# The preparation of the odd mixer, moved from a block of its own into the input projection ahead of it

## The chip, the cores and the metric

The kernel runs on one NeuronCore of a Trainium2 chip. The metric is the device time of one execution in microseconds (us), the median of several runs.

## The reference, cut to what matters

A trunk of two layers is stepped once for 576 tokens: one prompt of 512 and eight samples of 8. Each layer is a feed-forward half step, a mixer and another feed-forward half step. The mixer of the second layer, the odd one, is the place of the change. Its input projection `h @ w_in_odd` gives queries, keys, values and output gates for two kinds of heads, and in 24 further columns a low-rank input of the decays and the pre-activations of two gates:

```
q, k, v, gk_lr, z = _split(pc, C_WIDTHS)
gk = log_sigmoid(gk_lr @ w_gk2 + b_gk) / 16              # log decays, summed over each chunk
o_c = (_rms(gla(q, k, v, gk)) * gain_c) * silu(z)
q, k, v, i_in, f_in, o_in = _split(pd, D_WIDTHS)
f = cumsum(log_sigmoid(f_in + b_f));  m_t = max(log f_t + m_{t-1}, i_t)   # running sum and maximum
o_d = sigmoid(o_in) * (_rms(mlstm(q, k, v, i_in + b_i, f, m)) * gain_d)
```

All of it is fp32.

## The kernel before, in words

Features lie on the 128 partitions and the T = 576 tokens along the free dimension. `build` calls a chain of program blocks. `dense_chain` (L496) runs matrix products stage after stage in one block. After it come `prepare_odd` (L2865) and `odd_mixer` (L3085), each a block of its own (`nc.cleanup_on_exit()`, `nc.Block()`), and a second `dense_chain`. No instruction of a block starts before every engine, SyncE's DMA queue among them, has left the block before.

**A dense stage.** An output tile of 128 features is a unit of one or more pieces; a piece is one transfer of weights (128x1024). A product of fp32 accuracy is made of three passes: ScalarE copies the weights rounded (`split_high`, L161), VectorE subtracts to get the rest (`split_low`, L165), and TensorE multiplies low by high, high by low, high by high (L902, L904, L906), two matmuls of 288 columns each, over eight 128-row slices. The last stage is `proj_odd`, the input projection: 25 tiles, of which tile 24 (`NARROW`) holds the 24 further columns. Its first five tiles are made side by side of 288 tokens (10 pieces), the other 20 whole (20 pieces). Each engine's program is one loop over the pieces: in step i, VectorE first copies the tile that ended with piece i-1 out of PSUM (`copy_out`, L1242), then ScalarE and VectorE split the weights of piece i+2, whose place is free once piece i-1 has ended. TensorE waits at a unit for the copy of the unit three tiles back. Two units of TensorE's work therefore lie between the end of a piece and the use of what is split then.

**What else runs in the stage.** `Modulation` makes the shift, scale and gate vectors of the next sublayer: 16 transfers `w_mod` of 768 KB on SyncE's queue, from the fifth piece on, and a product after each of 16 pieces (L117), in psum banks 6 and 7. SyncE's queue runs through the transfers in order and waits at each for the place that it fills.

**`prepare_odd`.** SyncE fetches `w_gk2` (16 KB), the mixer's constants (1440 KB: masks, selections, and `resets`, the ones with zeros at which a running sum starts anew) and the samples' `m0` (L2898 to L2900). ScalarE makes silu of four tiles and sigmoid of four others (L2913, L2914; 128x2304 each), then the log-sigmoid of the forget gate as Abs, Exp, Ln (L2917 to L2921), each of the last two with an ACT_TABLE_LOAD. VectorE copies the gates' rows, makes the running sum and the running maximum (two scans of 4x576) and from them the mixer's rows. TensorE makes the inputs of the log decays (L2949: four matmuls, two tiles). For each of these two tiles in turn, VectorE shifts it (L3017), ScalarE runs Abs, Exp, Ln (L2924 to L2928), VectorE ends the log-sigmoid, scales it and makes two scans (L3020 to L3027). At the end ScalarE makes two exponentials of rows, TensorE turns rows into columns (L2954, L2956) and ScalarE copies these out (L2935, L2939).

**`odd_mixer`** takes four chunks of 128 tokens and one for the samples. TensorE's order is front(0), front(1), weights(0), outputs(0), weights(1), then for each chunk its rest and the next one's front. A front is eight transposes, fourteen products that use the constants and rows of 4 partitions, and some of 64 partitions.

## Time and profile before

| | before |
|---|---|
| median of 3 runs, us | 2833.3 (2832.71 to 2843.31) |
| the profiled execution's own time, us | 2840.6 |
| its span, first to last instruction, us | 2838.8 |
| granted TensorE clock, mean | 0.942 |
| busy share PE, PEld, DVE, ACT, POOL | 93%, 87%, 59%, 37%, 23% |
| from the last matmul of the projection to the first of the mixer, us | 2203.77 to 2246.43 |

PE is TensorE's matmul, PEld its weight load, DVE VectorE, ACT ScalarE, POOL GpSimd, SP SyncE. PEclk is the granted TensorE clock: 1.00 is 2.4 GHz and 0.50 is 1.2 GHz, the two levels that it has. The other engines' instructions keep their length at either level. In a timeline a row is one or several like instructions: start, time covered, engine, line, operation, out<-in, count, and in brackets how long the engine had been idle and what ended that.

### The profile page before, as it was taken

Reading aid. Unit: us, or ns where it says so; the run is one execution under the profiler, and the core shown is the slowest. Engines: PE = TensorE matmul, PEld = TensorE weight load, DVE = VectorE, ACT = ScalarE, POOL = GpSimd, SP = SyncE. Lnnn points to the kernel's source line nnn. Section 1 sums busy time; section 2 is a strip of 40 time slices with the busy share of each in tenths; the row PEclk is TensorE's granted clock in tenths of the full one; section 3 lists DMA queues with packets and bytes.
Section 4 is the critical chain, followed back from the end, with each engine's and each line's share of the span. In section 5 each row is a group of like instructions: output and inputs, shape, how many; then the busy total and the mean of one; then the engine's idle time right before and its main releaser. Section 6 shows DMA issues by size and latency. Waiting matters only on the chain. (4 is left out here: it accounts for less than half of the span.)

```text
span 2838.8 us, 52254 instructions
## 1 busy us (share of the span) xinstructions
PE 2638.0 (93%) x22592; PEld 2460.6 (87%) x22592; DVE 1688.3 (59%) x2345; ACT 1051.5 (37%) x1527; POOL 667.1 (23%) x502
## 2 busy tenths in 40 slices
PE   3999999999689998999999999999999498999998
PEld 0999988899378876899998999998889378999998
DVE  2787725743466646678952678852622355787824
ACT  2444414322533322444432544432421433544522
POOL 1356201000011021245510045510000121256401
PEclk7999999999679987999999999999999579999999
DMA  6233455621100013322255422255651104232324
GB/s 250 75 97 98 147 191 160 244 86 47 58 2 3 3 55 123 119 75 90 92 175 167 133 75 96 95 175 171 212 191 53 51 20 127 75 97 91 100 82 128
DMA packets 79757, 307.30 MB, mean 108 GB/s; under 512 B 9112, under 2 KB 14120, under 8 KB 77992
## 3 DMA queue, kind: packets, MB, share of 16 engines
q1 hardware_dynamic: 79528, 303.96, 32.4%
q8 instruction: 178, 2.92, 0.4%
q14 instruction: 51, 0.42, 0.0%
HBM read 293.19 MB, written 10.74 MB: 107 GB/s over the span
## 5 line engine op out<-in xcount | busy, mean ns | idle before, releaser
L165 DVE TENSOR_TENSOR weights_r<-work,weights_r 128x1024 fp32r<-128x1024 f32 (+2 forms) x300 | 392.7, 1309 | 292.9 <-ACT weights_r L161 292.3
L161 ACT ACTIVATE weights_r<-work 128x1024 fp32r<-128x1024 f32 (+2 forms) x300 | 291.4, 972 | 551.8 <-PE banks L906 334.4
L904 PE MATMUL banks<-low_r,weights_r 128*128 128x288 f32 (+2 forms) x1112 | 270.7, 300 | 0.0
L799 POOL TENSOR_TENSOR rows<-rows,consts 128x288 f32<-128x288 f32 (+3 forms) x64 | 88.7, 1386 | 692.8 <-ACT consts L1018 688.3
L902 PE MATMUL banks<-low_r,weights_r 128*128 128x288 f32 (+2 forms) x800 | 207.9, 307 | 26.4 <-DVE weights_r L165 17.7
L816 PE MATMUL banks<-h_r,weights_r 128*128 128x288 f32 x780 | 230.6, 296 | 0.9 <-DVE weights_r L165 0.9
L817 PE MATMUL banks<-big_r,weights_r 128*128 128x288 f32 x780 | 229.9, 295 | 0.0
L818 PE MATMUL banks<-h_r,weights_r 128*128 128x288 f32 x780 | 229.8, 295 | 0.0
L902 PE MATMUL banks<-h_r,weights_r 128*128 128x288 f32 (+1 forms) x824 | 198.2, 302 | 23.1 <-DVE big_r L423 22.8
L904 PE MATMUL banks<-big_r,weights_r 128*128 128x288 f32 (+2 forms) x848 | 210.0, 298 | 0.0
L165 DVE TENSOR_TENSOR ring_r<-work,ring_r 128x1024 fp32r<-128x1024 f32 (+1 forms) x108 | 148.7, 1377 | 93.8 <-ACT ring_r L161 93.4
L906 PE MATMUL banks<-low_r,weights_r 128*128 128x288 f32 (+2 forms) x800 | 201.7, 299 | 0.0
L906 PE MATMUL banks<-h_r,weights_r 128*128 128x288 f32 (+1 forms) x824 | 194.7, 298 | 0.0
L904 PEld LDWEIGHTS banks<-low_r,weights_r 128*128 128x128 f32 x1112 | 191.7, 191 | 0.2
L902 PEld LDWEIGHTS banks<-low_r,weights_r 128*128 128x128 f32 x800 | 139.7, 192 | 49.7 <-issue 25.0
L818 PE MATMUL banks<-low_r,weights_r 128*128 128x288 f32 x584 | 173.6, 297 | 0.0
L817 PE MATMUL banks<-low_r,weights_r 128*128 128x288 f32 x584 | 173.2, 297 | 0.0
L902 PEld LDWEIGHTS banks<-h_r,weights_r 128*128 128x128 f32 x824 | 138.9, 189 | 38.9 <-issue 31.0
L816 PE MATMUL banks<-low_r,weights_r 128*128 128x288 f32 x584 | 172.3, 295 | 0.0
L161 ACT ACTIVATE ring_r<-work 128x1024 fp32r<-128x1024 f32 (+1 forms) x108 | 104.1, 963 | 147.9 <-PE banks L818 111.0
L816 PEld LDWEIGHTS banks<-h_r,weights_r 128*128 128x128 f32 x780 | 146.6, 188 | 1.6 <-DVE weights_r L165 1.6
L818 PEld LDWEIGHTS banks<-h_r,weights_r 128*128 128x128 f32 x780 | 146.9, 188 | 0.0
(557 smaller groups left out, 7160.7 us busy)
## 6 DMA issues: line engine op xcount, KB each, us to landing
work<-w_ff_dram SPq DMA_DIRECT2D x118, 512.0 KB, 3.7
h<-w_mod_dram SPq DMA_DIRECT2D x48, 768.0 KB, 5.2
work<-w_down_dram SPq DMA_DIRECT2D x66, 512.0 KB, 3.6
consts<-w_ff_dram SPq DMA_DIRECT2D x58, 512.0 KB, 3.6
work<-w_mod_dram SPq DMA_DIRECT2D x32, 768.0 KB, 9.3
work<-w_in_even_dram SPq DMA_DIRECT2D x24, 512.0 KB, 3.8
big_buf<-w_mod_dram SPq DMA_DIRECT2D x16, 768.0 KB, 6.0
consts<-w_down_dram SPq DMA_DIRECT2D x22, 512.0 KB, 3.6
```

Of the source, the lines that this page charges most:

```text
L161: return act.activation(high, raw, ACT.Copy)
L165: return engine.tensor_tensor(low, raw, high.bitcast(F32), ALU.subtract)
L799: pool.tensor_tensor(k.rows[:, c], k.rows[:, c], k.square[:, c], ALU.add).then_inc(added, 1)
L816: pe.matmul(out, low[:, w], x_high, start=j == 0, stop=False)
L817: pe.matmul(out, high[:, w], x_low, start=False, stop=False)
L818: last = pe.matmul(out, high[:, w], x_high, start=False, stop=j == KT // 2 - 1)
L902: pe.matmul(out[a], low[:, w], x[a][0], start=begins, stop=False)
L904: pe.matmul(out[a], high[:, w], x[a][1], start=False, stop=False)
L906: last = pe.matmul(out[a], high[:, w], x[a][0], start=False, stop=closes)
```

## The change

`prepare_odd` is gone, and with it one block. Its work is spread over steps 12 to 24 of the projection's 30 pieces, by a class `OddGates`. The narrow tile is made first (`row` starts at `NARROW`), so that it is there after piece 5. Silu and sigmoid are made tile by tile as ScalarE takes the tile out of PSUM (`gate_out`), in place of VectorE's copy. The two log-decay tiles are handled as one of 1152 columns in ScalarE's three operations, and share psum pair 3 with each other. The resets are made by GpSimd. `w_gk2` and `m0` are fetched early in the stage, behind a wait for the last residual add of the stage before (`taken`). The constants are fetched in two parts at the end of the transfers, the second once the last piece that used their place has ended; the mixer's first product that reads them waits for both. The second slot of the modulation's weights is moved elsewhere in SBUF.

```diff
...
-        self.row = [(m + (UP_FIRST if kind == "up" else 0)) % n for m in range(n)]
+        self.row = [(m + {"up": UP_FIRST, "proj_odd": NARROW}.get(kind, 0)) % n for m in range(n)]
...
+class OddGates:
...
+        self.x, self.soft_x = k.arena[:, 6 * D:6 * D + 2 * T], at(11, 2)
+        self.col_rows, self.resets16, self.resets = at(13), at(14), at(15)
+        self.lf, self.soft, self.fsum = row(at(16)), row(at(17)), row(at(18))
...
+    def load(self, sp):
+        sp.dma_start(self.w2, self.k.io["w_gk2"]).then_inc(self.loaded, 16)
+        sp.dma_start(self.m0, self.k.io["mm_in"]).then_inc(self.loaded, 16)
+    def store(self, sp):
+        sp.wait_ge(*self.q.after("dve", "m_last"))
+        sp.dma_start(self.k.io["mm_p_out"], self.m[:, TP - 1:TP]).then_inc(self.stored, 16)
+        sp.dma_start(self.k.io["mm_s_out"], self.m_last).then_inc(self.stored, 16)
+        sp.wait_ge(self.stored, 32)
...
+    def constants(self, pool):
+        for resets, of_prompt in ((self.resets16, 16), (self.resets, CH)):
+            pool.memset(resets, 1.0).then_inc(self.filled, 1)
...
+    def gate_product(self, pe, i):
+        did, after = self.q.did, self.q.after
+        if i == 0:
+            pe.wait_ge(self.loaded, 32)
+            pe.wait_ge(self.mod.finished, 2)
+        else:
+            pe.wait_ge(*after("dve", "x0"))
+        for a in range(2):
+            last = pe.matmul(self.k.psum_pair(3)[:, a, 0:HALF], self.w2[:, i * P:(i + 1) * P],
+                             self.narrow[0:16, a * HALF:(a + 1) * HALF], start=True, stop=True)
+        last.then_inc(*did("pe", f"gk{i}"))
+    def columns(self, pe):
+        k = self.k
+        pe.wait_ge(*self.q.after("act", "ends_e"))
+        pe.wait_ge(*self.q.after("dve", "x1"))
+        for c in range(NCH):
+            pe.transpose(k.psum[6][:, c * P:(c + 1) * P], self.col_rows[:, c * P:(c + 1) * P], k.mask("ident"))
+        for g in range(2):
+            last = pe.matmul(k.psum[7][64 * g:64 * g + 64, 0:P], self.col_rows[:, TP:T], k.mask("ident"),
+                             start=True, stop=True)
+        last.then_inc(*self.q.did("pe", "cols"))
...
+    def soft_of_f(self, act):
+        did, after = self.q.did, self.q.after
+        act.wait_ge(*after("dve", "fg"))
+        act.activation(self.soft, self.fg, ACT.Abs).then_inc(self.abs_f, 1)
+        act.wait_ge(self.abs_f, 1)
+        act.activation(self.soft, self.soft, ACT.Exp, scale=-1.0).then_inc(self.exp_f, 1)
+        act.wait_ge(self.exp_f, 1)
+        act.activation(self.soft, self.soft, ACT.Ln, bias=1.0).then_inc(*did("act", "soft_f"))
...
+    def ends(self, act):
+        did, after = self.q.did, self.q.after
+        act.wait_ge(*after("dve", "e_s"))
+        act.activation(self.col_rows[32:36, :], self.floor, ACT.Exp, scale=-2.0).then_inc(*did("act", "ends_m"))
+        act.activation(self.col_rows[0:4, :], self.e_row, ACT.Exp).then_inc(*did("act", "ends_e"))
+    def soft_of_x(self, act):
+        did, after = self.q.did, self.q.after
+        act.wait_ge(*after("dve", "x1"))
+        act.activation(self.soft_x, self.x, ACT.Abs).then_inc(self.abs_x, 1)
+        act.wait_ge(self.abs_x, 1)
+        act.activation(self.soft_x, self.soft_x, ACT.Exp, scale=-1.0).then_inc(self.exp_x, 1)
+        act.wait_ge(self.exp_x, 1)
+        act.activation(self.soft_x, self.soft_x, ACT.Ln, bias=1.0).then_inc(*did("act", "soft_x"))
...
+    def column_copies(self, act):
+        k = self.k
+        act.wait_ge(*self.q.after("pe", "cols"))
...
+    def gates(self, dve):
+        did, after = self.q.did, self.q.after
+        dve.tensor_copy(self.fg, self.narrow[64:68])
+        dve.tensor_copy(self.ig, self.narrow[32:36]).then_inc(*did("dve", "gates"))
+        dve.wait_ge(*after("dve", "gates"))
+        dve.tensor_scalar(self.fg, self.fg, self.k.par("b_f")[0:4], None, ALU.add).then_inc(*did("dve", "fg"))
...
+    def running_maximum(self, dve):
+        did, after = self.q.did, self.q.after
+        tt, w = dve.tensor_tensor, lambda name: dve.wait_ge(*after("dve", name))
+        firsts = slice(TP, T, TS)
+        dve.wait_ge(*after("act", "soft_f"))
+        w("lf0")
+        tt(self.lf, self.lf, self.soft, ALU.subtract).then_inc(*did("dve", "lf"))
...
+    def rows_of_m(self, dve):
...
+    def shifted(self, dve, i):
+        dve.wait_ge(*self.q.after("pe", f"gk{i}"))
+        dve.tensor_scalar(self.x[:, i * T:(i + 1) * T].rearrange("p (a t) -> p a t", a=2),
+                          two_halves(self.k.psum_pair(3), HALF), self.k.par("b_gk")[:, i:i + 1], None, ALU.add)\
+            .then_inc(*self.q.did("dve", f"x{i}"))
+    def log_decays(self, dve):
+        did, after = self.q.did, self.q.after
+        dve.wait_ge(*after("act", "soft_x"))
+        dve.scalar_tensor_tensor(out=self.x, in0=self.x, scalar=0.0, in1=self.soft_x, op0=ALU.min, op1=ALU.subtract)\
+            .then_inc(*did("dve", "s1"))
+        dve.wait_ge(*after("dve", "s1"))
+        dve.tensor_scalar(self.x, self.x, 1.0 / 16.0, None, ALU.mult).then_inc(*did("dve", "s2"))
+    def sums(self, dve, tile, resets, name):
+        dve.wait_ge(*self.q.after("dve", "s2"))
+        for i in range(2):
+            dve.tensor_tensor_scan(self.k.big_buf[:, (tile + i) * T:(tile + i + 1) * T], resets, self.x[:, i * T:(i + 1) * T],
+                                   0.0, ALU.mult, ALU.add).then_inc(*self.q.did("dve", f"{name}{i}"))
...
+class MixerConstants:
+    def __init__(self, k):
+        self.k, self.landed = k, k.nc.alloc_semaphore("constants_landed")
+    def load(self, sp, lo, hi):
+        sp.dma_start(self.k.consts[:, lo:hi], self.k.io["consts_in"][:, lo:hi]).then_inc(self.landed, 16)
...
-                mods.append((stage, Modulation(k, s, stage.sublayer + 1, [room[:, 0:MOD_W], arena_slot],
+                slot = arena_slot if stage.kind == "proj_even" else k.arena[:, LOW + 8 * T:LOW + 8 * T + MOD_W]
+                mods.append((stage, Modulation(k, s, stage.sublayer + 1, [room[:, 0:MOD_W], slot],
...
+        gates_at = (lambda n: odd[0].first + n) if odd else (lambda n: None)
+        gating = {m: f for tile, f in ((Z_C, ACT.Silu), (O_D, ACT.Sigmoid)) for m in range(tile, tile + 4)}
+        by_act = [u for stage in odd for u in stage.units if u.m in gating]
+        by_dve = [u for stage in odd for u in stage.units if u.m not in gating]
+        def emptied(engine, stage, m, sides):
+            u = max((stage.of[m, a] for a in sides), key=lambda v: v.nth)
+            if u in by_act:
+                engine.wait_ge(gated_out, by_act.index(u) + 1)
+            else:
+                engine.wait_ge(evacuated, by_dve.index(u) + 1)
...
-            return k.psum_pair(u.m % (2 if u.kind in TAIL_SKEW else 3))
+            return k.psum_pair(u.stage.row.index(u.m) % (2 if u.kind in TAIL_SKEW else 3))
...
+                    if odd_gates and i == gates_at(4):
+                        sp.wait_ge(taken, [v for v in units if v.kind in TAIL_SKEW][-1].nth + 1)
+                        odd_gates.load(sp)
...
+                if constants:
+                    for done in [load for i, load in enumerate(loads) if i % RAW == RAW - 1][-1].freed:
+                        sp.wait_ge(*done)
+                    constants.load(sp, 0, D)
+                    sp.wait_ge(piece_done, max(i for i, piece in enumerate(pieces) if piece.place == SPLIT - 1) + 1)
+                    constants.load(sp, D, USED_CONST - T)
+                if odd_gates:
+                    odd_gates.store(sp)
...
+                    if stage.kind == "proj_odd":
+                        odd_gates.constants(pool)
...
-                        pe.wait_ge(evacuated, max(stage.of[u.m - 3, a].nth for a in u.sides) + 1)
+                    if u.kind == "proj_odd" and stage.row.index(u.m) >= 3:
+                        emptied(pe, stage, stage.row[stage.row.index(u.m) - 3], u.sides)
...
+                        if odd_gates and i in (gates_at(19), gates_at(20)):
+                            if i == gates_at(19):
+                                emptied(pe, stage, NARROW, (0, 1))
+                            odd_gates.gate_product(pe, i - gates_at(19))
+                        if odd_gates and i == gates_at(22):
+                            odd_gates.columns(pe)
...
+                def gate_out(u):
+                    act.wait_ge(piece_done, u.pieces[-1][0] + 1)
+                    c = u.cols()
+                    act.activation(shaped(u, k.big_buf[:, u.m * T + c.start:u.m * T + c.stop]), product_of(u, u.pieces[0]),
+                                   gating[u.m]).then_inc(gated_out, 1)
...
+                    if u in by_act:
+                        gate_out(u)
...
+                    if odd_gates:
+                        if i == gates_at(12):
+                            odd_gates.soft_of_f(act)
+                        if i == gates_at(14):
+                            odd_gates.ends(act)
+                        if i == gates_at(21):
+                            odd_gates.soft_of_x(act)
+                        if i == gates_at(23):
+                            odd_gates.column_copies(act)
...
-                    if u and u.kind == "proj_odd":
+                    if u in by_dve:
...
+                    if odd_gates:
+                        if i == gates_at(12):
+                            emptied(dve, odd[0], NARROW, (0, 1))
+                            odd_gates.gates(dve)
+                        if i == gates_at(13):
+                            odd_gates.running_maximum(dve)
+                        if i == gates_at(14):
+                            odd_gates.rows_of_m(dve)
+                        if i in (gates_at(20), gates_at(21)):
+                            odd_gates.shifted(dve, i - gates_at(20))
+                        if i == gates_at(22):
+                            odd_gates.log_decays(dve)
+                        if i == gates_at(23):
+                            odd_gates.sums(dve, B_C, odd_gates.resets, "b")
+                        if i == gates_at(24):
+                            odd_gates.sums(dve, B16, odd_gates.resets16, "b16_")
...
-def prepare_odd(k):
...
+                    pe.wait_ge(constants.landed, 32)
...
+    constants = MixerConstants(k)
...
-    prepare_odd(k)
+                    Stage("proj_odd", 4, EDGES)], constants=constants)
     early = EarlyWeights(k, "w_out_odd")
-    odd_mixer(k, early)
+    odd_mixer(k, early, constants)
...
```

The bodies left out of `OddGates` are those of `prepare_odd`, in the same order. `emptied` waits for ScalarE's or VectorE's emptying of a tile, whichever engine takes it.

TensorE, in the projection: `gate_product(0)` (L563, after piece 19). L1150, L1152 and L1154 are the three passes, once L902, L904 and L906.

```order
L1152 MATMUL banks<-low_r,weights_r 128x288 x2
L1154 MATMUL banks<-h_r,weights_r 128x288 x2
L563 MATMUL banks<-big_buf,gated 128x288 x2
L1150 MATMUL banks<-h_r,weights_r 128x288 x2
L1152 MATMUL banks<-low_r,weights_r 128x288 x2
```

The same two matmuls stand again after piece 20, and the six of `columns` after piece 22; ahead of it the order before had them between the two blocks:

```order
L2943 UNCONDITIONAL_BRANCH
L2949 MATMUL banks<-big_buf,work 128x288 x4
L2954 MATMUL banks<-base,work 128x128 x4
L2956 MATMUL banks<-base,work 64x128 x2
L2895 UNCONDITIONAL_BRANCH
```

All ten matmuls now stand inside TensorE's stream of the projection.

ScalarE, steps 12 to 18 of the projection: the gate work (L581 to L591), silu of the four tiles (L1300) and the weights' rounding between them (L161).

```order
L581 ACTIVATE work<-consts 4x576
L583 ACT_TABLE_LOAD
L583 ACTIVATE work<-work 4x576
L585 ACT_TABLE_LOAD
L585 ACTIVATE work<-work 4x576
L161 ACTIVATE ring_r<-consts 128x1024
L161 ACTIVATE weights_r<-work 128x1024
L590 ACT_TABLE_LOAD
L590 ACTIVATE work<-consts 4x576
L591 ACTIVATE work<-work 4x576
L1300 ACT_TABLE_LOAD
L1300 ACTIVATE big_buf<-banks 128x576
```

Before, only L161 stood there: the rounding of piece 15 now stands behind the gate's three operations.

SyncE's queue, at the start of the projection (the fifth piece's transfer, then):

```order
L954 DMA work<-w_in_odd_dram 128x1024
L538 DMA gated<-w_gk_dram 16x256
L539 DMA work<-mm_in_dram 4x8
L106 DMA big_buf<-w_mod_dram 128x1536
L954 DMA work<-w_in_odd_dram 128x1024
```

The first `w_mod` transfer has moved behind a wait and two small transfers.

## Rows read from the trace of the kernel before

**Rows 1.** Windows by stage: projection, preparation, mixer's start; busy (xcount), PEclk, DMA share, GB/s.

```profile
2050.00:2204.00 154.00, 153.49 (x1169) 143.45 (x1167) 46.47 (x54) 27.30 (x27) 0.00 (x0) 1.00 0.37 128
2204.00:2246.00 42.00, 5.94 (x16) 3.50 (x16) 20.55 (x38) 23.60 (x25) 0.58 (x1) 0.54 0.10 36
2246.00:2284.00 38.00, 37.05 (x264) 29.67 (x264) 10.78 (x34) 11.76 (x25) 13.47 (x34) 0.52 0.18 56
```

**Rows 2.** Timeline of TensorE: start, us, engine, line, operation, idle before.

```profile
2190.65 0.43 PE L906 MATMUL banks<-h_r,ring_r 128*128 128x288 f32 x2
...
2203.34 0.43 PE L906 MATMUL banks<-h_r,weights_r 128*128 128x288 f32 x2
2212.05 4.20 PE L2949 MATMUL banks<-big_buf,work 16*128 16x288 f32 x8 [8.28 <-DMA work<-mm_in_dram]
2243.47 1.11 PE L2954 MATMUL banks<-base,work 128*128 128x128 f32 x4 [27.21 <-ACT work L2932]
2244.51 0.70 PE L2956 MATMUL banks<-base,work 128*64 128x128 f32 x4
2246.43 1.94 PE L3266 MATMUL banks<-base,big_buf 128*128 128x128 f32 x8 [1.22 <-PEq L2890]
...
2257.98 1.92 PE L3266 MATMUL banks<-base,big_buf 128*128 128x128 f32 x8
...
2269.70 2.55 PE L3251 MATMUL banks<-work 64*128 64x128 f32 x64
```

**Rows 3.** Timeline of VectorE, same stretch.

```profile
2203.81 0.76 DVE L1242 COPY big_buf<-banks 128x576 f32<-128x576 f32 x1 [5.58 <-PE banks L906]
...
2243.31 1.33 DVE L3027 TENSOR_TENSOR_SCAN big_buf<-work 128x576 f32<-128x576 f32 x1
```

**Rows 4.** Timeline of ScalarE, same stretch.

```profile
2207.15 2.12 ACT L2913 ACTIVATE big_buf<-big_buf 128x2304 f32<-128x2304 f32 x1
...
2227.40 1.28 ACT L2926 ACT_TABLE_LOAD   x1
2228.70 0.68 ACT L2926 ACTIVATE work<-work 128x576 f32<-128x576 f32 x1
```

**Rows 5.** Groups of instructions by shape, 2120 to 2204: the projection's second part.

```profile
L1242 DVE COPY big_buf<-banks 128x576 f32<-128x576 f32 x14 | 10.6, 758 | 60.7 <-PE banks L906 60.7
...
L165 DVE TENSOR_TENSOR weights_r<-work,weights_r 128x1024 fp32r<-128x1024 f32 x8 | 9.8, 1226 | 3.1 <-ACT weights_r L161 3.1
L161 ACT ACTIVATE weights_r<-work 128x1024 fp32r<-128x1024 f32 x8 | 8.5, 1060 | 41.1 <-PE banks L906 41.1
```

**Rows 6.** Timeline of SyncE's queue, start of projection and start of preparation.

```profile
2026.46 0.33 SPq L719 DMA_DIRECT2D work<-w_in_odd_dram  x1
2026.84 0.43 SPq L106 DMA_DIRECT2D big_buf<-w_mod_dram  x1
...
2206.24 0.41 SPq L2899 DMA_DIRECT2D consts<-consts_in_dram  x1
```

**Rows 7.** Timeline of VectorE, the last residual add of the down stage.

```profile
2026.95 0.21 DVE L1189 TENSOR_TENSOR work<-work,gated 128x64 f32<-128x64 f32 x1
```

**Rows 8.** Timeline of TensorE, the first modulation product of the projection.

```profile
2034.77 0.83 PE L117 MATMUL banks<-big_buf,cs 128*9 128x384 f32 x8 [1.21 <-DMA big_buf<-w_mod_dram]
```

**Rows 9.** DMA issues, 2180 to 2300: KB each, median us to landing.

```profile
consts<-consts_in_dram SPq DMA_DIRECT2D x1, 1440.0 KB, 6.3
```

**Rows 10.** Windows of one or two us: three places where TensorE's clock falls.

```profile
2014.00:2016.00 2.00, 0.18 (x2) 0.16 (x2) 1.50 (x2) 0.46 (x1) 0.00 (x0) 1.00 0.00 0
...
2017.00:2018.00 1.00, 1.00 (x6) 1.00 (x6) 0.44 (x2) 0.96 (x2) 0.00 (x0) 0.50 0.77 279
...
2208.00:2209.00 1.00, 0.00 (x0) 0.00 (x0) 0.93 (x3) 1.00 (x1) 0.00 (x0) 0.50 0.68 265
2288.00:2289.00 1.00, 1.00 (x7) 0.76 (x7) 1.00 (x5) 0.99 (x1) 0.00 (x0) 1.00 0.00 0
...
2290.00:2291.00 1.00, 1.00 (x7) 1.00 (x6) 0.62 (x4) 0.41 (x1) 0.00 (x0) 0.50 0.00 0
```

265 lines of the change are left out of this document (93 added, 172 removed).

## The prediction

> **What bounds the kernel now.** I read the granted clock and the busy shares first: TensorE is busy 93% of the span, so a change pays where TensorE stands still or runs slowly. Then I read the windows by stage [rows 1]. In the projection's second part TensorE is busy 153.49 of 154 us at full clock, with VectorE at 46 us and ScalarE at 27: TensorE alone bounds it. In the 42 us of `prepare_odd` it is busy 5.94 us, and in the first 38 us of the mixer 37.05 us, at a clock of 0.52. The timeline of TensorE [rows 2] gives the borders: the last matmul of the projection ends at 2203.34 + 0.43 = 2203.77, the mixer's first starts at 2246.43. Those 42.66 us are a chain through ScalarE and VectorE, with three ends: log decays, running maximum, columns. Nothing but this chain holds the mixer back.
>
> **What goes.** The whole preparation leaves the path. What stays is one passage from block to block. Before, VectorE copied the last tile from 2203.81 for 0.76 us [rows 3], and SyncE could start its first transfers some 1.3 us after that copy's end (L2899, the second of them, went out at 2206.24 [rows 6]). The passage from the last matmul to the next block's start is therefore some 2.1 us, and the mixer's first matmul should start at about 2205.9. In the new block the last tile is taken by ScalarE with a sigmoid, 0.68 us for 128x576 [rows 4], in place of the 0.76: equal. **Minus 42.66, plus 2.1: -40.5 us.**
>
> **What TensorE takes over.** Four matmuls of `gate_product` took 4.20 us and the six of `columns` 1.74 us (2243.47 to 2244.51 + 0.70) [rows 2], both at the clock of 0.50 [rows 10]. In the projection the clock is 1.00 [rows 1], so half: 2.1 + 0.9. **+3.0 us**; the bounds are 2.9 and, if the clock dropped for them, 5.9. I take the lower end, since the projection's own small products (nine rows wide, L117) ran among the others in a stretch at 1.00.
>
> **Breaks in TensorE's stream.** Three insertions with a wait each. No row shows such a break. It is bounded by nothing below, and above by the 1.21 us that TensorE stood for a late operand [rows 8]; I take 0.1 each, near the lower end, since here the operands are early: x0 is there some 3 us after piece 19, while piece 20 runs 6.3 us. **+0.3 us** (0 to 3.6).
>
> **SyncE's queue.** The fetch of `w_gk2` and `m0` waits for the last residual add and stands ahead of the first `w_mod` transfer. Before, that transfer went out at 2026.84 [rows 6], 0.38 us after the fifth piece's. The last add ends at 2026.95 + 0.21 = 2027.16 [rows 7]. After it come two issues of some 0.35 us (the distance of two issues, 2026.46 to 2026.84, is 0.38), so the first `w_mod` goes out at 2027.9, 1.1 us later. And TensorE did wait for exactly this transfer: 1.21 us at its first modulation product [rows 8]. Nothing covers it. **+1.1 us** (0, if another transfer is what is really slow; 3.3, if three products inherit the delay). The queue's other new work, the constants, comes after the last weights.
>
> **The constants.** 1440 KB landed in 6.3 us [rows 9]. Now 512 KB go first, and 640 KB after the last piece that used the place `ring_r`. That piece ends at 2190.65 + 0.43 [rows 2], two tiles (12.7 us) ahead of the end, so at less than 6.3 us per part both lie in SBUF 6 us before the mixer starts. The stores of m are behind them in the queue and have the same 12 us. **0.** If that cover were gone, a mixer that waits costs up to 6.3 us less the passage of 2.1.
>
> **ScalarE and VectorE.** A tile takes 6.35 us of TensorE (12.69 us from the last `ring_r` matmul to the last of all, over two tiles [rows 2]). The weights split in step i need 1.06 us on ScalarE and 1.23 us on VectorE [rows 5] and are used 12.7 us after the step begins: 10.4 us to spare. The heaviest step is 21, the log-sigmoid of 1152 columns: by the lengths for 576 and 2304 columns (0.68 and 2.12 us [rows 4]) some 1.16 us an operation, three of them and two table loads of 1.28 make 6.0, behind a start about 3.5 us into the tile. The next step's rounding is then some 3 us late: a third of what is to spare. The forget gate's step 12 (4.6 us, starting 4 us in) is lighter. Over steps 12 to 24 ScalarE gets some 18 us of new work on 14, in 82 us; VectorE at most the preparation's 20.55 us [rows 1] on 26 (1.23 and 0.76 a tile [rows 5]), and is spared eight copies. GpSimd's fills are early. **0.** The same holds for the one table load at the mixer's head (1.28 us): TensorE has 2269.70 - 2246.43 = 23.3 us of its own fronts [rows 2] before it needs the first result that hangs on it.
>
> **The clock at the mixer's head.** Before, the mixer started at 0.50 and stayed there for most of 38 us [rows 1] although TensorE was busy. Now it starts 2.1 us after dense work at 1.00. How long does that last? Three rows bound it [rows 10]: a standstill of 1.8 us at 2014 was followed by 0.50 at 2017; after the end of the projection it was 0.50 in the window of 2208, 4 us on; and the same kind of front as at the mixer's start, with TensorE busy without a gap, had 1.00 at 2288 and 0.50 at 2290. So 0 to 3 us of the first front run at full rate, and each saves one. **-1.0 us** (0 to -3; to -5 if the clock also returns earlier).
>
> The Trainium skill, "TensorE: Matmul & The Clock Gate", section "What's actually happening", has the clock follow from how busy TensorE has been recently. By that rule a mixer entered warm, and busy 97% of the time, would keep the full clock, which is the second case below. The trace does not agree so far: at 2290 the clock fell under a fully busy TensorE.
>
> **Sum.** -40.5 + 3.0 + 0.3 + 1.1 - 1.0 = -37.1 us. Against the profiled execution's own 2840.6 us that is 2803.5; it lay 7.3 us above the median of the runs, which themselves reach from 2832.7 to 2843.3. Against the median: 2833.3 - 37.1 = **2796 us**, -1.3%. A measurement of this kernel can tell about 0.5% (14 us) from no change.
>
> **The rivals.**
> *The mixer's head stays warm* (0.07). A front takes 11.55 us now (2246.43 to 2257.98 [rows 2]), all at half clock. At full clock the 37.05 us of the head would shrink by nearly half; waits for ScalarE and VectorE would come in, so I count 16 us: 2797.2 without the clock term, less 16, **2781 us**. For it: the gap shrinks from 42.7 to 2.1 us. Against it: the fall at 2290.
> *The new steps hold TensorE up a little* (0.06): ScalarE waits for VectorE and VectorE for ScalarE inside one step, which before happened only for the split. If each of the 13 steps loses 1 us, **2809 us**. Against it: the 10.4 us to spare.
> *Slower, or no faster: the chain moves in whole* (0.03). The place is ScalarE's loop, where the rounding of piece i+2 is queued behind a log-sigmoid that waits for VectorE, which waits for TensorE's product. It decides once a step's chain takes over 12.7 us; if every link of the old 40.5 us chain then stalls TensorE, the time is 2833.3 + 3.0 + 0.3 + 1.1 = **2838 us**, and if the clock falls in the stalls so that two or three tiles run at half rate (6.35 us each) 2851 us. Against it: ScalarE's work in these steps would have to be nearly four times the 32 us that I count before it made up 82 + 37 us.
> *The block's end is not free* (0.04): the change does not do all that it says, because the second part of the constants or the stores end late, or the passage grows with the semaphores to clear. A landing of 6.3 us that starts only at the end would give **2802 us**.
>
> **How the numbers follow.** My forecast has 0.80. Its bounds, from 2796: down to 2792 with the clock's -5, up to 2804 with TensorE's added work at half clock, the breaks and the queue at their upper ends together. The runs before differ by 10 us among themselves, of which a median of three can catch some. The range 2785 to 2806 takes in these and the last rival; it leaves out the warm head, the held-up steps and the slower case, 0.16. Faster by over 0.5% (below 2819): all but the third rival and a tail of the second, 0.95. Within 0.5%: 0.03. Slower by over 0.5%: 0.02, the third rival with the clock's fall.
>
> **What would show it.** TensorE's pause between the projection's last matmul and the mixer's first: 2.1 us. Ten extra matmuls in the projection at 1.00, in all 3 us, each with under 0.5 us of idle before it. TensorE's first modulation product waiting 2.3 us instead of 1.2. ScalarE's L161 in steps 13 and 22 a few us later after TensorE's release, and no idle of TensorE that ends on L161 or L165 in the projection's second half. The wait for `constants.landed` at zero. The first windows of the mixer at 1.00, then 0.50 within 3 us. Wrong would be: a pause of over 5 us between the blocks, a projection longer by more than 8 us, or a mixer whose first front takes under 8 us.

## The result, and the profile after the change

| | before | after |
|---|---|---|
| median, us | 2834.92 (2832.71 to 2843.31, 4 runs) | 2801.26 (2794.63 to 2805.64, 4 runs) |
| the profiled execution's own time, us | 2840.6 | 2797.84 |
| its span, us | 2838.8 | 2796.1 |
| granted TensorE clock, mean | 0.942 | 0.953 |
| from the last matmul of the projection to the first of the mixer, us | 42.66 | 2.09 |

The ratio is 0.9877 [0.9853, 0.9901], so the change takes off 1.2% (28 to 42 us). The forecast was 2796 us with a range from 2785 to 2806, and faster at 0.95. The same kernel timed once more in five rounds (experiment 1) came to 2796.26 us and 0.9852 [0.9824, 0.9881]. The prediction holds in sign, in size and in nearly every step; one term, SyncE's queue, does not, and the clock's term is right by luck.

The head of the page after the change:

```profile
span 2796.1 us, 52231 instructions
...
PE 2626.2 (94%) x22592; PEld 2451.0 (88%) x22592; DVE 1702.4 (61%) x2333; ACT 1049.3 (38%) x1529; POOL 663.5 (24%) x507
...
PE   3999999999689998999999999999999998999998
...
PEclk7999999999779997999999999999999789999999
```

The same two rows of the page before:

```profile
PE   3999999999689998999999999999999498999998
PEclk7999999999679987999999999999999579999999
```

In the row of TensorE the 4 that stood in the 32nd slice of before is gone, and the clock's 5 and 7 there have become 7 and 8. TensorE is still busy nearly everywhere, so what the change gained is one hole.

The windows by stage, as [rows 1] has them for before: 154 us of the projection, then the first 38 us of the mixer.

```profile
2046.00:2200.00 154.00, 154.00 (x1161) 142.43 (x1161) 59.78 (x79) 47.18 (x52) 0.00 (x0) 1.00 0.40 135
2204.00:2242.00 38.00, 36.59 (x272) 29.25 (x273) 11.44 (x34) 12.92 (x26) 13.67 (x34) 0.55 0.18 56
```

The first line shows that the moved work fits. VectorE went from 46.47 to 59.78 us in 154, ScalarE from 27.30 to 47.18, and TensorE had no idle time at all. The second shows that the mixer's head is hardly better than before: clock 0.55 for 0.52.

The timeline of TensorE: the two insertions of `gate_product`, that of `columns`, and the passage into the mixer.

```profile
2135.09 0.43 PE L1154 MATMUL banks<-h_r,weights_r 128*128 128x288 f32 x2
2135.45 1.23 PE L563 MATMUL banks<-big_buf,gated 16*128 16x288 f32 x4
2136.61 0.53 PE L1150 MATMUL banks<-h_r,weights_r 128*128 128x288 f32 x2
...
2143.16 1.23 PE L563 MATMUL banks<-big_buf,gated 16*128 16x288 f32 x4
2144.33 0.53 PE L1150 MATMUL banks<-h_r,ring_r 128*128 128x288 f32 x2
...
2157.16 0.60 PE L572 MATMUL banks<-base,work 128*128 128x128 f32 x4
2157.68 0.44 PE L574 MATMUL banks<-base,work 128*64 128x128 f32 x4
2158.05 0.53 PE L1150 MATMUL banks<-h_r,weights_r 128*128 128x288 f32 x2
...
2202.37 0.43 PE L1154 MATMUL banks<-h_r,weights_r 128*128 128x288 f32 x2
2204.89 1.24 PE L3362 MATMUL banks<-base,big_buf 128*128 128x128 f32 x8 [2.09 <-PEq L738]
```

No insertion has an idle time in brackets. From the start of an insertion to the next pass are 1.16, 1.17 and 0.89 us, 3.2 in all. The last row has the passage: the matmul ends at 2202.80, and after 2.09 us, ended by TensorE's own queue, the mixer starts.

The timeline of ScalarE, the heaviest step and the passage:

```profile
2146.41 1.17 ACT L596 ACTIVATE work<-work 128x1152 f32<-128x1152 f32 x1 [2.02 <-DVE work L673]
2147.59 1.28 ACT L598 ACT_TABLE_LOAD   x1
2148.89 1.17 ACT L598 ACTIVATE work<-work 128x1152 f32<-128x1152 f32 x1
2150.07 1.28 ACT L600 ACT_TABLE_LOAD   x1
2151.37 1.17 ACT L600 ACTIVATE work<-work 128x1152 f32<-128x1152 f32 x1
2152.44 1.04 ACT L161 ACTIVATE ring_r<-consts 128x1024 fp32r<-128x1024 f32 x1
...
2202.83 0.65 ACT L1300 ACTIVATE big_buf<-banks 128x576 f32<-128x576 f32 x1 [5.69 <-PE banks L1154]
2204.85 1.28 ACT L3546 ACT_TABLE_LOAD   x1 [1.37 <-PEq L738]
```

The log-sigmoid of 1152 columns takes 2146.41 to 2152.54 = 6.1 us (6.0 were forecast), 1.17 an operation (1.16). The weights rounded behind it at 2152.44 are first used at 2164.51.

### The profile page after: what moved, and what is told of

It reads as the page before. It is cut to its first block and busy times, and to the rows that moved or that the text cites. A ratio compares the mean times of both kernels' runs of the same rounds, so it can differ in the third digit from the quotient of the medians.

```text
span 2796.1 us, 52231 instructions
## 1 busy us (share of the span) xinstructions
PE 2626.2 (94%) x22592; PEld 2451.0 (88%) x22592; DVE 1702.4 (61%) x2333; ACT 1049.3 (38%) x1529; POOL 663.5 (24%) x507
## 5 line engine op out<-in xcount | busy, mean ns | idle before, releaser
L165 DVE TENSOR_TENSOR weights_r<-work,weights_r 128x1024 fp32r<-128x1024 f32 (+2 forms) x300 | 398.5, 1329 | 303.6 <-ACT weights_r L161 302.8
L161 ACT ACTIVATE weights_r<-work 128x1024 fp32r<-128x1024 f32 (+2 forms) x300 | 291.3, 972 | 525.8 <-PE banks L1154 307.9
L1152 PE MATMUL banks<-low_r,weights_r 128*128 128x288 f32 (+2 forms) x1112 | 270.6, 300 | 0.0
L1150 PE MATMUL banks<-low_r,weights_r 128*128 128x288 f32 (+2 forms) x800 | 208.2, 307 | 27.0 <-DVE weights_r L165 18.1
L1150 PE MATMUL banks<-h_r,weights_r 128*128 128x288 f32 (+1 forms) x824 | 198.2, 302 | 23.7 <-DVE big_r L423 22.8
L1152 PE MATMUL banks<-big_r,weights_r 128*128 128x288 f32 (+2 forms) x848 | 209.9, 298 | 0.0
L1154 PE MATMUL banks<-low_r,weights_r 128*128 128x288 f32 (+2 forms) x800 | 201.8, 299 | 0.0
L1154 PE MATMUL banks<-h_r,weights_r 128*128 128x288 f32 (+1 forms) x824 | 194.4, 298 | 0.0
L1152 PEld LDWEIGHTS banks<-low_r,weights_r 128*128 128x128 f32 x1112 | 191.5, 191 | 0.2
L1150 PEld LDWEIGHTS banks<-low_r,weights_r 128*128 128x128 f32 x800 | 139.8, 192 | 50.5 <-issue 25.0
L1150 PEld LDWEIGHTS banks<-h_r,weights_r 128*128 128x128 f32 x824 | 138.5, 189 | 40.3 <-issue 30.9
L161 ACT ACTIVATE ring_r<-work 128x1024 fp32r<-128x1024 f32 (+1 forms) x108 | 104.0, 963 | 146.8 <-PE banks L1066 109.9
```

Of the source, the lines that this page charges most:

```text
L161: return act.activation(high, raw, ACT.Copy)
L165: return engine.tensor_tensor(low, raw, high.bitcast(F32), ALU.subtract)
L1150: pe.matmul(out[a], low[:, w], x[a][0], start=begins, stop=False)
L1152: pe.matmul(out[a], high[:, w], x[a][1], start=False, stop=False)
L1154: last = pe.matmul(out[a], high[:, w], x[a][0], start=False, stop=closes)
```

## The same execution in five stretches

Each profile was cut at five marks: the 1.82 us stall of TensorE just ahead of the projection, the last matmul of the projection, the mixer's first, its stall of 3.84 us before the samples' last products, and the first product of the output stage. The last column runs from there to TensorE's last matmul of the span. All in us, each found in the timelines.

| kernel | stall stands at | projection | passage | mixer to the stall | to the output stage | rest |
|---|---|---|---|---|---|---|
| before | 2015.9 | 187.9 | 42.7 | 89.4 | 30.3 | 462.4 |
| after | 2012.1 | 190.7 | 2.1 | 88.4 | 29.9 | 462.7 |
| 1 the change again | 2010.5 | 190.4 | 2.1 | 88.0 | 31.1 | 462.5 |
| 2 before, kept warm | 2019.2 | 187.5 | 41.9 | 86.9 | 29.9 | 467.3 |
| 3 rows of 128 | 2015.3 | 190.7 | 2.1 | 69.2 | 29.7 | 462.6 |
| 4 gate weights later | 2015.1 | 193.5 | 2.1 | 87.0 | 29.9 | 462.4 |
| 5 ScalarE plus 6 | 2015.2 | 192.0 | 2.1 | 86.7 | 29.9 | 463.4 |
| 6 ScalarE plus 18 | 2009.2 | 201.9 | 2.1 | 89.5 | 31.0 | 462.6 |
| 7 constants behind all | 2003.5 | 191.5 | 5.8 | 84.9 | 30.5 | 462.5 |
| 8 gates by tile only | 2011.7 | 187.1 | 38.0 | 92.4 | 30.7 | 462.9 |
| 9 rows of 128, timed | 2011.9 | 191.4 | 2.1 | 70.2 | 29.9 | 462.4 |
| 10 before, rows of 128 | 2017.2 | 188.0 | 42.7 | 67.9 | 30.6 | 463.0 |

The first column is the price of chance. The instructions ahead of that stall are the same in all of them, and its end moves over 15.7 us. Much of this is the clock: TensorE's busy time at 0.50 ahead of the stall adds up to 140 us in the kernel before and to 107 in kernel 7, which comes there first (all twelve: 107 to 140 us). Why the clock differs there stays open. Of the 42.7 us between the two profiled spans, 3.7 lie there and are no gain. The rest: +2.8 in the projection, -40.6 in the passage, -1.0 in the mixer, and -0.1 behind it.

## The experiments

Theory A is the prediction's: the gain is the passage, and the rest is small terms beside it. The questions are whether each small term is what I said, and where the mixer's clock comes from. Kernels 2, 8 and 10 start from the kernel before, the others from the changed one.

**1. The change again**, no edit, five rounds.

> The changed kernel once more, in five rounds. The two profiles differ by 42.7 us of span; laid side by side, -40.6 us lie in the passage from the projection to the mixer, +2.8 in the projection, -1.0 in the mixer, -0.4 behind it, and -3.7 us ahead of the projection, where no instruction was changed. If those last 3.7 us are chance between executions, the true difference is the -39 of the changed places (2834.9 - 39 = 2796) and the ratio of the runs closes in on 0.986. If the 2801 of the first four runs is the truth, some 5 us are lost in a place that the one profile does not show, and the ratio stays at 0.988.

Measured: 2796.26 us (2791.78 to 2802.37), before 2837.05, ratio 0.9852 [0.9824, 0.9881]. The ratio went to the 0.986 of the first case, not to 0.988, though its interval holds both. The stretches repeat within 0.4 us up to the mixer's stall.

**2. The passage filled with products**, to keep the clock up.

```
 (prepare_odd, TensorE, between L2949 and the columns)
+                for _ in range(56):
+                    pe.matmul(k.psum[6][:, 0:2 * P], k.mask("ident"), k.base[:, 0:2 * P], start=True, stop=True)
```

> The kernel before, with 56 dense products (128x256 fp32) into an unused bank on TensorE while the preparation's chain runs on the other engines, so that TensorE enters the mixer at 1.00. They compute nothing that is used. Theory A (my forecast's clock term: warmth at the door is worth 0 to 3 us, since the front's own products bring the clock down): the chain and so the passage stay at 42.7 us, the clock is 1.00 at the mixer's first matmul and 0.50 within 5 us, and from the mixer's first matmul to the last transposes of the samples (89.4 us before) it takes 86 to 89 us. Rival (the fall in the changed kernel came from the 2.1 us pause, not from the front): with a pause of only 1.2 us the clock stays up through the first fronts, which then take 6 to 8 us in place of 11.5 each, and the stretch takes under 80 us.

Measured: the mixer entered at 1.00 and took 86.9 us, 2.5 less than before. Its first products ran at the full rate. Then TensorE, now early, waited 2.18 us for ScalarE's first result (until 2256.31), and the clock fell at 2254.66, 6.1 us in and half a us into this wait, not within the 5 us of theory A. It stayed at 0.50 for 27.3 us. So a warm entry does not give the 16 us that a warm head would. Whether it gives anything is not shown: without any edit of its products this stretch takes 84.9 to 92.4 us in the table, and the shortest of them, kernel 7, entered it at 0.50. The 2844.7 us of the whole are one run, of which 5 us lie in the last column.

**3. and 9. The row products over 128 partitions.** In a front, eight of twelve products of the logarithms, and two behind them, contract over the 4 rows fm, w and a. The edit gives them 128 partitions, of which 124 are zero (the 128 rows are cleared once by GpSimd); the sums are the same.

```
-    rfm, rw, a_row = (k.mrows[:, i * T:(i + 1) * T] for i in range(3))
+    rfm, rw, a_row = (k.mrows_all[:, i * T:(i + 1) * T] for i in range(3))
...
-                            mm(out, k.select(h)[0:4], rfm[:, here], start=False, stop=False)
-                            last = mm(out, a_row[:, here], k.select(h)[0:4], start=False)
+                            mm(out, k.select(h), rfm[:, here], start=False, stop=False)
+                            last = mm(out, a_row[:, here], k.select(h), start=False)
```

> The changed kernel, with the mixer's products over 4 partitions (the rows of the running maximum with the selections) taken over all 128, the other 124 holding zeros. Same columns, same passes, same results. Theory A (the clock falls in a front because its products use few partitions of the array): a front keeps 1.00, takes 6 us in place of 11.5, and the mixer from its first matmul to the samples' transposes shrinks from 88.4 us to 75 to 80. Rival (it is the zeros or the fp32 passes or the many short products that bring the clock down, not the number of partitions addressed): clock and length stay as they are, within 2 us.

> The changed kernel with the products of the rows fm, w and a of the odd mixer taken over 128 partitions (124 of them zero) instead of 4, as in the earlier single look at it (2781.6 us, mixer 69.2 us), now timed. Theory A (the products over 4 partitions are what brings the clock down in the mixer, and the gain of 19 us there is real and repeats): mixer 68 to 71 us, gap 2.1 us, time 2774 to 2785 us, ratio to the kernel before 0.976 to 0.983, about 0.007 below the ratio of the changed kernel alone (0.985). Theory B (the earlier look had the clock by chance): the mixer comes back to 84 to 89 us and the time to 2793 to 2802, ratio about 0.986.

Measured: 2781.56 us and a mixer of 69.2 us in the single run; then 2778.12 us (2771.63 to 2780.62, 6 runs) beside 2833.95 before, ratio 0.9787 [0.976, 0.9813], mixer 70.2 us. Theory A holds; in the single run it held with more than the forecast (69.2 us for 75 to 80). This is the fastest version here.

**10. The same edit on the kernel before.**

> The kernel before, with the same edit of the mixer's row products (128 partitions, 124 of them zero) and nothing of the change, so the 42.7 us passage and its fall of the clock stay. Theory A (the fall in the mixer comes of its own row products, whatever the clock was at its entry): after a cold entry the clock is back at 1.00 within the first front and stays; mixer 70 to 76 us instead of 89.4, passage 42 to 43 us, time 2815 to 2824 us, ratio to the kernel before 0.992 to 0.996. Rival (the full clock of the mixer needs the warm entry that the change gives): the mixer keeps 0.50 over its fronts, 84 to 90 us, time 2832 to 2842 us, ratio 1.00.

Measured: 2818.72 us (2812.12 to 2823.22, 5 runs), ratio 0.9934 [0.9907, 0.9961], passage 42.7 us, mixer 67.9 us. The rival falls: no warm entry is needed, and the mixer is even below theory A's 70 to 76 us. Within the intervals the two edits do not touch each other's gain, since 0.9852 x 0.9934 = 0.9787 is the ratio of both together. The windows of this mixer from its cold entry on:

```profile
2248.00:2252.00 4.00, 4.00 (x20) 4.00 (x20) 1.09 (x3) 0.73 (x2) 4.00 (x9) 0.50 0.78 274
2252.00:2256.00 4.00, 2.87 (x26) 2.71 (x25) 1.32 (x6) 2.84 (x6) 1.96 (x5) 0.90 0.84 252
2256.00:2260.00 4.00, 4.00 (x38) 3.69 (x36) 1.42 (x4) 1.36 (x3) 3.18 (x8) 1.00 0.00 0
```

and those of the changed kernel, warm entry and rows of 4:

```profile
2204.00:2208.00 4.00, 3.11 (x15) 2.69 (x16) 1.19 (x3) 2.22 (x3) 3.15 (x9) 0.70 0.54 160
2208.00:2212.00 4.00, 4.00 (x14) 2.98 (x13) 0.50 (x3) 1.58 (x4) 3.24 (x8) 0.50 1.03 350
2212.00:2236.00 24.00, 23.48 (x151) 18.68 (x150) 7.55 (x24) 6.60 (x15) 5.90 (x15) 0.50 0.02 3
```

TensorE is busy 23.48 of 24 us in the last line and stays at 0.50; in kernel 10 the same front, entered at 0.50, is at 0.90 in its second window and at 1.00 in its third. The stretch to the mixer's stall in one window, before and in kernel 10:

```profile
2246.43:2335.82 89.39, 84.62 (x741) 68.60 (x741) 41.65 (x126) 34.52 (x71) 24.09 (x55) 0.71 0.09 28
2247.82:2315.71 67.89, 58.95 (x740) 50.15 (x740) 40.71 (x126) 33.86 (x71) 24.62 (x55) 0.95 0.12 37
```

Not all of the gain is the clock's. The timeline of TensorE in the kernel before, at 1.00, one group of three products:

```profile
2285.89 0.39 PE L3251 MATMUL banks<-consts,base 128*128 128x128 f32 x2
2286.21 0.48 PE L3251 MATMUL banks<-work,consts 4*128 4x128 f32 x2
2286.54 0.38 PE L3251 MATMUL banks<-consts,work 4*128 4x128 f32 x2
2286.85 0.49 PE L3251 MATMUL banks<-consts,base 128*128 128x128 f32 x2
```

and in kernel 10, also at 1.00:

```profile
2273.22 0.39 PE L3253 MATMUL banks<-consts,base 128*128 128x128 f32 x2
2273.44 0.39 PE L3253 MATMUL banks<-work,consts 128*128 128x128 f32 x2
2273.67 0.39 PE L3253 MATMUL banks<-consts,work 128*128 128x128 f32 x2
2273.89 0.39 PE L3253 MATMUL banks<-consts,base 128*128 128x128 f32 x2
```

From one group to the next are 0.96 us with rows of 4 and 0.67 with rows of 128; at 0.50 it is 1.71 (after, from 2205.92 to 2207.63) and 1.28 (kernel 10, from 2249.55 to 2250.83). So some 0.3 to 0.4 us of each of the 16 groups come from the shapes at equal clock, an estimate of 5 to 7 us. A second way gives less: if TensorE's busy time at 0.50 in the stretch is counted half, 60.0 us are left before and 56.4 in kernel 10, so the shapes are 4 us of the 21.5. The halved time falls from 24.6 to 2.5 us, so the clock gives 22, and TensorE's waits give 4 of that back (4.8 to 8.9 us). Either way most of the gain is the clock's. I had expected all of it from the clock.

The Trainium skill, "TensorE: Matmul & The Clock Gate", section "LDWEIGHTS (loading the stationary operand)", says that loading weights takes a time set by their columns, the same for 32 rows as for 128. The traces agree: one load of these takes 0.18 to 0.19 us with 4 rows and with 128, both at 1.00. What differs is the distance of the matmuls. With 128 rows each starts 0.11 us behind the one before. With rows of 4 three of a group's six distances are 0.20 to 0.21 us: the two at a change between 128 and 4 rows, and the one behind the first of them. The edit took away the few rows and these changes at once. So what holds the clock at 0.50, few rows or the stream that stops at each change, is not separated by any run here.

**4. The gate weights fetched later**, six pieces on, so that nothing stands ahead of the first `w_mod` transfer.

```
-                    if odd_gates and i == gates_at(4):
+                    if odd_gates and i == gates_at(10):
```

> The changed kernel, with the fetch of w_gk2 and m0 moved from the fifth to the eleventh piece of the projection, away from the first modulation weights. Theory A (my forecast's queue term of 1.1 us): the first modulation transfer goes out 0.4 us behind the fifth piece's as before, and from the projection's first stall to its last matmul (190.7 us in the changed kernel, 187.9 before) it takes 1.1 us less, 189.6. Rival (the delay was taken up by other stalls: TensorE stood 1.64 us in the projection's first 20 us in the changed kernel and 1.49 before): no more than 0.3 us less.

Measured: 2801.91 us, and TensorE's first modulation product waited 1.87 us, longer and not shorter than the 0.45 of the changed kernel. Neither theory had that. The projection took 193.5 us, 2.8 more. Part of it is chance: the clock fell after the stall ahead of the projection (0.57 in the four us behind it, 1.00 in the changed kernel) and again after the wait of 1.87 us. This run by itself decides nothing; all profiles together say more, below.

**5. and 6. ScalarE made late on purpose**, in the heaviest step, by repeating its first operation (1.17 us) 5 and 15 times.

```
-        act.activation(self.soft_x, self.x, ACT.Abs).then_inc(self.abs_x, 1)
-        act.wait_ge(self.abs_x, 1)
+        for j in range(16):
+            act.activation(self.soft_x, self.x, ACT.Abs).then_inc(self.abs_x, 1)
+            act.wait_ge(self.abs_x, j + 1)
```

> The changed kernel with the Abs of the log decays (128x1152, 1.17 us on ScalarE) done six times instead of once, in the heaviest step: 6.0 us more on ScalarE between a tile's end and the rounding of the weights two tiles on. Theory A (my forecast's slack; the profile of the change leaves 10.0 us between the end of the split of piece 24 at 2154.7 and its first use at 2164.7): nothing, the projection from its first stall to its last matmul stays at 190.4 to 190.7 us. Rival (the new steps sit near the edge): TensorE waits some us at the tile after next.

> The same with the Abs done sixteen times, 17.9 us more. Theory A: the 10.0 us to spare are used up and the rest shows, a wait of 8 us of TensorE on VectorE's split of one tile, and 1 to 3 us more because the clock falls in the wait: the projection takes 199 to 202 us. Rival (the chain has more or less to spare than the timeline says, because VectorE's share moves along with it): a wait that differs from 8 us by more than 2.

Measured with 6 us: 2801.16 us, and in the projection's second half no wait of TensorE. The projection took 192.0 us, outside theory A's 190.4 to 190.7. The 1.3 us over the changed kernel's lie at the start, where TensorE waited 1.35 and 0.47 us for `w_mod` and the clock fell behind the stall; kernel 7, where it fell too, took 191.5. With 18 us: 2808.26 us and a projection of 201.9 us. Its timeline of TensorE:

```profile
2170.18 0.82 PE L1151 MATMUL banks<-h_r,ring_r 128*128 128x288 f32 x2 [8.18 <-DVE ring_r L165]
```

A delay of 17.6 us (15 x 1.17) came out as a wait of 8.2, so some 9.4 us of it were hidden, and the 8 us expected are there. The changed kernel's own rows say 9.8: the split of that piece ends at 2154.74 and is first used at 2164.51. The slack is there, and the heaviest step takes little of it: that piece could be rounded from 2151.0 on, when VectorE too found the tile before it ended, and was from 2152.44.

**7. The constants' second part behind the last piece**, without cover.

```
-                    sp.wait_ge(piece_done, max(i for i, piece in enumerate(pieces) if piece.place == SPLIT - 1) + 1)
+                    sp.wait_ge(piece_done, total)
```

> The changed kernel with the second part of the constants (640 KB) fetched after the last piece of the projection instead of two tiles ahead. Theory A (my forecast: the prefetch is what keeps the block's end free, and without it a mixer waits up to 6.3 us less the passage): the transfer starts at the last matmul, lands some 3 to 5 us later, TensorE has 2.1 us of passage and 1.0 us of transposes before it needs them, so it waits 0 to 3 us in the first front, beside the states' 2 MB that share the queue. The mixer takes 88 to 91 us, in place of 88.0 to 88.4. Rival (the stores of m behind the constants, on whose end SyncE waits, hold the whole block open): the pause between the blocks grows from 2.1 to 5 us or more.

Measured: passage 5.8 us. The timeline of TensorE, and then of SyncE's queue:

```profile
2200.74 1.94 PE L3362 MATMUL banks<-base,big_buf 128*128 128x128 f32 x8 [5.78 <-PEq L738]
```

```profile
2194.99 0.33 SPq L711 DMA_DIRECT2D consts<-consts_in_dram  x1
2195.36 0.33 SPq L543 DMA_DIRECT2D mm_p_out_dram<-consts  x1
2195.74 0.30 SPq L544 DMA_DIRECT2D mm_s_out_dram<-work  x1
2200.70 0.37 SPq L3234 DMA_DIRECT2D h<-gla_in_dram  x1
```

No product waits for `constants.landed`. It is the block's end that waits, for the transfer (4.0 us from issue to landing) and the two stores behind it: 5.78 - 2.09 = 3.7 us. Which of the two ends last was not separated. That is the rival's form, and nearly its price (6.3 - 2.1 = 4.2). That the kernel as a whole was fast, 2790.6 us, is the first column of the table: its projection began 8.7 us earlier than the changed kernel's.

**8. Only the gates tile by tile**, `prepare_odd` left in its place.

```
+                    if u in by_act:
+                        gate_out(u)
...
-                    if u and u.kind == "proj_odd":
+                    if u in by_dve:
...
-                act.activation(big(Z_C, 4), big(Z_C, 4), ACT.Silu).then_inc(*did("act", "silu_z"))
-                act.activation(big(O_D, 4), big(O_D, 4), ACT.Sigmoid).then_inc(*did("act", "sig_o"))
```

> The kernel before, with only one part of the change: silu and sigmoid are made as ScalarE takes each tile out of PSUM, and the two operations of 128x2304 are gone from the preparation. The rest of the preparation stays a block of its own. From the timeline before: the forget gate's Abs waited for ScalarE until 2212.6, while its input was ready at 2208.1. Theory A: the chain starts 4.5 us earlier, and its end with it: the pause between the blocks' large work falls from 42.7 to 38.2 us, so that of the 40.5 us saved 4.5 belong to the gates by tile and 36 to the move of the chain. Rival (TensorE's first products wait for w_gk2 until 2212 and set the chain's end through the log decays): the pause stays within 1 us of 42.7.

Measured: a passage of 38.0 us. Its timeline of TensorE:

```profile
2207.17 4.20 PE L2968 MATMUL banks<-big_buf,work 16*128 16x288 f32 x8 [8.44 <-DMA work<-mm_in_dram]
2233.79 1.11 PE L2973 MATMUL banks<-base,work 128*128 128x128 f32 x4 [22.42 <-ACT work L2951]
...
2236.75 1.94 PE L3285 MATMUL banks<-base,big_buf 128*128 128x128 f32 x8 [1.22 <-PEq L2911]
```

So 4.7 of the 40.6 us are the eight tiles of silu and sigmoid, and 36 the chain of the decays. Of [rows 2], the wait of 27.21 us on ScalarE has become 22.42, and the one of 8.28 at the start stays. The whole took 2834.93 us beside 2833.64, so the 4.7 us do not show in it: in this one run the mixer took 92.4 us, of which the clock was at 0.50 for 58 us (52 in the kernel before).

## Why the prediction was right, and where it was not

**What goes: right.** -40.5 was forecast, -40.57 measured (42.66 to 2.09), and 2.1 in all six further profiles of the changed kernel in which the constants are in their place. The last tile's sigmoid is 0.65 us long for the copy's 0.76, as assumed.

**What TensorE takes over, and the breaks: right.** +3.0 and +0.3 were forecast; the insertions show 3.2, all at 1.00. L563 takes 2.3 of it for 2.1, the columns 0.89 for 0.9. That counts to the start of the next pass. Up to the projection's end the growth is 3.7 us, from its last modulation product on (88.0 us for 84.3). So beside the 3.0 the three breaks come to some 0.7 us and not 0.3, small as forecast, but more than 0.1 each.

**SyncE's queue: wrong.** +1.1 was forecast. The step assumed that a transfer issued later lands later. It was issued 0.75 us later (11.72 us behind the stall for 10.97), but TensorE was released 6.3 us behind the issue for 7.9, and went on 18.0 us behind the stall for 18.9. Its waits in the projection:

```profile
2016.10 0.40 PE L1150 MATMUL banks<-low_r,weights_r 128*128 128x288 f32 x1 [0.54 <-DVE weights_r L165]
...
2025.81 0.72 PE L353 MATMUL banks<-rows,base 128*128 128x288 f32 x2 [0.65 <-POOL rows L1047]
...
2030.16 0.83 PE L117 MATMUL banks<-big_buf,cs 128*9 128x384 f32 x8 [0.45 <-DMA big_buf<-w_mod_dram]
```

That is 1.64 us in all for 1.49 before, 1.21 at the first `w_mod` [rows 8] and 0.28 at a later one (2059.99). Over twelve profiles the wait for the first `w_mod` is 0.71, 0.91, 1.21, 1.42 and 1.87 us where nothing stands ahead of the transfer, and 0.23, 0.38, 0.45, 0.53, 0.58, 0.90 and 1.35 us where the two small transfers do. There is no sign of the +1.1. The DMA engines are some 90% busy in this stretch (0.88 in 2024 to 2034 before, 0.91 in 2020 to 2030 after). That the landing is therefore set by what they carry, and not by an issue 0.75 us earlier, is argued and not tested by itself.

The stretch itself varies with the clock: after the stall of 1.82 us it fell in five profiles and stayed in seven. Compared like with like, the projection with the change takes 190.4 to 191.4 us for 187.1 and 187.5 where the clock stayed, and 191.5 and 192.0 for 187.9 and 188.0 where it fell (kernels 4 and 6 aside): +3.5 and +3.8. The forecast was 3.0 + 0.3 + 1.1 = 4.4, so it is high by the queue's term. The two traces first compared give only +2.8, because the clock fell in the one and not in the other.

**The constants: right, with the wrong price beside it.** Both parts land at the cost of nothing. Without the cover it is 3.7 us, as the block's end and not as the mixer's wait. The forecast had two prices for that, 6.3 - 2.1 = 4.2 here and the full 6.3 in its last rival; the measured one is near the first.

**ScalarE and VectorE: right for the projection.** 0, with 9.8 us left of the 12.7 in the trace and 9.4 by kernel 6. The step had the rounding in the heaviest step some 3 us late; it was 1.4 us late. Its cover of 23.3 us for the mixer's head was misread: TensorE needs ScalarE's first result within the first front, not after two. In the changed kernel the product that waits for it in kernel 9 starts at 2214.10, 9.2 us in, and ScalarE's result was there at 2212.55. So 1.6 us were to spare, not over 20, and the 0 held because the front ran at half clock.

**The clock at the mixer's head: the size is luck, the mechanism half right.** -1.0 was forecast and the mixer is 1.04 us shorter. But no such difference can be read here: with rows of 4 the stretch to the stall takes 89.4, 84.9 and 92.4 us where it was entered at 0.50 (before, 7 and 8) and 86.7 to 89.5 us where it was entered at 1.00 (after, 1, 2, 4, 5 and 6). What it takes follows how long the clock is at 0.50 in it, from 41 us in kernel 7 to 58 us in kernel 8, with TensorE's busy time, counted half where it is at 0.50, at 59.5 to 60.6 us in all nine. The clock fell 0.7 us in, within the 0 to 3 us of the forecast; in kernel 1 it was 2 us, in kernel 4 it was 6. What I took for the mixer's nature was the shape of its products.

By the rule of the Trainium skill, "TensorE: Matmul & The Clock Gate", section "What's actually happening", a busy TensorE keeps the full clock. The traces agree with it for rows of 128 (0.95 in the mean) and not for rows of 4 (0.50 at 23.48 us busy of 24), so the busy share of a profile alone does not tell the clock here.

**The sum.** -37.1 was forecast; without the queue it would have been -38.2. Measured are -42.7 less the 3.7 of chance ahead of the projection, -39.0, and by the ratios 1.2 and 1.5%, -35 and -42 us. The term that carries it, the passage, is right to 0.1 us; a difference of one us in the others is below what the runs can tell. Of the rivals, the warm head did not come about, neither in the changed kernel nor with a warm entry alone (kernel 2); held-up steps, the chain moved in whole and the block's end did not come about.

## What to carry to other kernels

A chain of small operations between two dense blocks costs its whole length; inside a dense stage it costs only what TensorE itself takes over, as long as each step's delay is shorter than the lead of the weights, which one deliberate delay measures. Where the granted clock is 0.50 under a busy TensorE, look for products over few partitions and try them widened with zeros: here one edit of a few lines gave nearly half as much again as the whole move. It was measured in this mixer alone. Transfers that fill a place late should stand ahead of the block's end by more than their own landing, because there it is the end of the block that waits for them.

## What was not expected of the hardware

**The shape of products and the clock.** It stood at 0.50 under products over 4 partitions with TensorE busy 98% (after, 2212 to 2236), and rose to 1.00 under the same products over 128 (kernel 10, 2252 to 2256). With rows of 4 it first rose 36 us into the mixer before, 35 in the changed kernel and 12 in kernel 1; with rows of 128 it rose 5 us into it in kernel 10.

**The same stall, two outcomes.** After the stall of 1.82 us ahead of the projection the clock fell in five of twelve profiles and stayed in seven. Behind the passage of 2.09 us it fell 0.2 to 2 us into the mixer (after and kernels 1, 3, 5, 6), or not in its first 5 us (kernels 4 and 9). There it fell 6.0 and 6.4 us in, each time during TensorE's first wait for ScalarE, as in kernel 2. What decides between the outcomes stays open.

**A front at full rate meets a new wait.** The timeline of TensorE in kernel 9:

```profile
2213.21 1.22 PE L3348 MATMUL banks<-big_buf 64*128 64x128 f32 x8 [3.60 <-ACT work L3563]
```

and those of GpSimd and ScalarE ahead of it:

```profile
2206.01 1.95 POOL L3315 MEMSET work<- 128x1088 f32 x2
...
2210.30 0.61 POOL L3279 TENSOR_TENSOR work<-big_buf 128x256 f32<-128x256 f32 x1
2210.95 0.42 ACT L3551 ACTIVATE work<-work 128x256 f32<-128x256 f32 x1 [3.34 <-POOL work L3279]
```

GpSimd is busy without a gap from 2205.37 to 2210.91, first with fills and then with products, and ScalarE stands 3.34 us for it before it makes what TensorE waits for. The table load on ScalarE (1.28 us) is over by 2206.66 and is not on this path. Behind fronts at half clock the path was hidden; here TensorE waits for it, and the clock falls once in this wait. Moving GpSimd's fills ahead of the mixer was not tried.

**A spread ahead of the change.** The same instructions ahead of the projection ended anywhere within 15.7 us in twelve profiles, more than a third of what the change gains. The largest single step, that of kernel 7, is between 1048 and 1082 us: TensorE, busy throughout, had the clock at 0.50 for 34 us in the kernel before and for 14 us in kernel 7. What sets that was not looked into.
